# Router logits from the raw residual with scaled weights, routing by pairwise comparison, three token tiles routed inside the last projection tile, and h2 made by GpSimd

## The reference

```python
x = x + gate1 * mixed                      # mixed = (merged branches) @ w_o
h2 = rms_norm(x, norm2_g) * (1 + scale2) + shift2
x = x + gate2 * hier_moe(h2, p)
# hier_moe(h):
gl = x @ w_rg + b_rg                       # 4 groups, top 1
el = x @ w_re + b_re                       # 16 experts, 4 in a group, top 2 of the chosen group
topv = topv / sum(topv); weights = gp_sel * topv
g = einsum('nd,edf->nef', x, w_e_gate); u = einsum('nd,edf->nef', x, w_e_up)
act = silu(g) * u * combine[:, :, None]
out = einsum('nef,efd->nd', act, w_e_down)
```

## Time and profile before

| | us |
|---|---|
| three runs | 738.91, 739.37, 739.41 (median 739.37) |
| profiled execution, first to last instruction (span) | 737.5 |
| last projection group ends, the add of its tile starts | 505.6 |
| `slot_i` written | 531.3 |
| first gathered tile transposed | 537.7 |
| high matmuls of slot 0, of slot 1 start | 540.8, 548.7 |

### The profile page before, as it was taken

The page is one execution under the profiler, slowest core; times in us unless marked ns, Lnnn a source line. Parts: engine busy times, 40 slices in busy tenths (PEclk is TensorE's granted clock), DMA queues, the critical chain, the costliest instruction groups (busy, mean ns, idle before and its releaser), DMA issues.

```text
span 737.5 us, 11172 instructions
## 1 busy us (share of the span) xinstructions
PE 703.8 (95%) x4440; PEld 611.4 (83%) x4440; DVE 544.1 (74%) x785; ACT 344.3 (47%) x454; POOL 201.3 (27%) x84
## 2 busy tenths in 40 slices
PE   5899999999999999999999999998989999999985
PEld 2499999999998899999999998886368888877752
DVE  3547999999768765955556563555799999888877
ACT  4552223433333444446365121134387888777622
POOL 4004321322200000000000000000239999797560
PEclk9999999999999999999999999999599999999998
DMA  9954145445625345512325326266958999999783
GB/s 321 377 169 141 59 172 172 172 172 173 218 83 114 31 120 123 116 61 61 111 64 166 114 71 217 80 245 218 412 195 335 394 406 404 393 357 361 262 283 144
DMA packets 75607, 149.10 MB, mean 202 GB/s; under 512 B 11302, under 2 KB 54626, under 8 KB 68836
## 3 DMA queue, kind: packets, MB, share of 16 engines
q1 hardware_dynamic: 61572, 125.28, 49.4%
q10 hardware_dynamic: 10096, 12.63, 4.8%
q0 software_dynamic: 3888, 10.49, 4.2%
HBM read 138.29 MB, written 20.05 MB: 215 GB/s over the span
## 4 chain that ended last, share of the span: by engine, by line
PE 76%; DMA 9%; DVE 4%; issue 3%; ACT 3%; POOL 2%; SPq 2%; POOLq 0%; DVEq 0%; ACTq 0%
PE psum L990 36%; PE psum L1241 8%; PE psum L1283 7%; PE psum L505 3%; PE psum L925 3%; PE psum L506 3%; PE psum L511 3%; DMA down_raw<-in_w_e_down 2%; DMA w_more<-in_w_ada 2%; PE psum L1188 2%; DMA xg<-h_d,slot_b 1%; PE psum L1432 1%; SPq L791 1%; PE psum L1118 1%; PE psum L1009 1%
## 5 line engine op out<-in xcount | busy, mean ns | idle before, releaser
L990 PE MATMUL psum<-hh,w_h 128*128 128x320 f32 x608 | 144.4, 319 | 0.2 <-issue 0.2
L990 PE MATMUL psum<-hh,w_l 128*128 128x320 f32 x608 | 138.5, 309 | 0.0
L990 PE MATMUL psum<-hl,w_h 128*128 128x320 f32 x608 | 138.4, 309 | 0.0
L2014 DVE SCALAR_TENSOR_TENSOR psum<-conv,taps,psum 128x760 f32<-128x760 f32 x103 | 104.5, 1015 | 3.5
L990 PEld LDWEIGHTS psum<-hh,w_h 128*128 128x128 f32 x608 | 99.8, 188 | 5.4 <-issue 3.1
L990 PEld LDWEIGHTS psum<-hl,w_h 128*128 128x128 f32 x608 | 101.6, 188 | 0.0
L990 PEld LDWEIGHTS psum<-hh,w_l 128*128 128x128 f32 x608 | 101.5, 188 | 0.0
L717 POOL TENSOR_TENSOR down_l<-down_raw,down_h 128x2048 fp32r<-128x2048 f32 x16 | 87.8, 5486 | 20.8 <-ACT down_h L1787 20.3
L683 POOL TENSOR_TENSOR ob<-obh,toff 128x260 bf16<-128x260 f32 x1 | 2.0, 1995 | 332.1 <-DVE obh L591 332.1
L2300 DVE TENSOR_TENSOR w_l<-w_raw,w_h 128x2048 fp32r<-128x2048 f32 x26 | 77.0, 2966 | 11.7 <-ACT w_h L1793 11.7
L917 POOL TENSOR_TENSOR w_l<-w_raw,w_h 128x2048 fp32r<-128x2048 f32 x9 | 41.8, 4640 | 144.1 <-ACT w_h L1468 144.1
(11 more groups left out here) (384 smaller groups left out, 1403.4 us busy)
## 6 DMA issues: line engine op xcount, KB each, us to landing
w_raw<-in_w_in SPq DMA_DIRECT2D x20, 1024.0 KB, 6.7
down_raw<-in_w_e_down SPq DMA_DIRECT2D x17, 1024.0 KB, 12.3
w_raw<-in_w_ada SPq DMA_DIRECT2D x16, 1024.0 KB, 9.2
w_raw<-in_w_e_gate SPq DMA_DIRECT2D x13, 1024.0 KB, 7.8
w_raw<-in_w_e_up SPq DMA_DIRECT2D x13, 1024.0 KB, 11.3
w_more<-in_w_ada SPq DMA_DIRECT2D x8, 1024.0 KB, 10.5
y_d<-yy ACTq DMA_DIRECT2D x15, 512.0 KB, 8.2
y_d<-in_x_sample SPq DMA_DIRECT2D x12, 512.0 KB, 8.1
```

Of the source, the lines that this page charges most:

```text
L990: mm = pe.matmul(psum[:, p + q, 0:HALF], w, r[:, k, q * HALF:(q + 1) * HALF], start=(k == 0 and x == 0), stop=(k == KT - 1 and x == 2))
L2014: ins = dve.scalar_tensor_tensor(out=after, in0=src, scalar=w, in1=before, op0=MUL, op1=ADD)
```

## The change

- Router logits come from the transposes of x2 itself. `wrs` is `wr` times the scale row (now loaded as a column for each partition), the shift row's share is worked out once for both token kinds (`shift_terms`, `shift_rows`, `lgc`), and rstd multiplies the finished logits (`scaled_logits`).
- h2 is made by POOL (times scale row, then plus shift row, 1024 columns each) with a pass of ACT between (times rstd, `h2_scale`). POOL stores the last of the five tiles itself, on its own queue, and both the first gather and SP's load of down weights 2 wait for that store.
- Ranks come from pairwise comparisons with a tie term (`choose`). Tiles 0 to 2 are routed during the last projection group, tiles 3 and 4 after it.
- The slot list is one matmul per pick with the token's number as value (`oav`, float32 words), no longer two columns.
- SP loads the down weights of slot 0 when all logits are done, those of slot 2 when the last h2 tile is stored, and those of slot 1 when the slots' row weights are done.
- POOL waits for gather 0 to land before it issues gather 1. PE transposes gather 1 between the high and the low matmuls of slot 0, no longer ahead of them, and the second half of gate2's spreading stands behind the transposes of gather 0.
- 11 `keep_clock` matmuls ahead of the logits are gone, and 2 are left of the 3 ahead of slot 0. The load of `norm_final_g` moves into slot 2.

```diff
+    def x2_out(act, t, q):
         if t >= 2:
             act.wait_ge(lgt_pe, t - 1)
+        act.wait_ge(h2_pe, 2 * t + q + 1)
+        act.activation(h2t[:, t % 2, 4 * q:4 * q + 4, :],
+                       psum[:, 5 + q, :].rearrange("p (k n) -> p k n", k=4), ACT.Copy).then_inc(h2_ev, 1)
...
+    def choose(dve, then, t0, t1):
+
+        n = t1 - t0
+        sets = lg[:, t0:t1, :].rearrange("p t (s e) -> p (t s) e", e=GE)
+        ahead = lead[:, 0:5 * n, :, :]
+        wide = [P, 5 * n, GE, GE]
+        then(dve.tensor_tensor(ahead, sets.unsqueeze(2).to_broadcast(wide), sets.unsqueeze(3).to_broadcast(wide), SUB))
+        flat_sets = lead[:, 0:5 * n, :, :].rearrange("p a i j -> p a (i j)")
+        then(dve.tensor_tensor(flat_sets, flat_sets,
+                               tau[:, :, :].rearrange("p i j -> p (i j)").unsqueeze(1).to_broadcast([P, 5 * n, GE * GE]),
+                               ALU.is_gt))
+        then(dve.tensor_reduce(rank[:, 0:n, :, :].rearrange("p t s e -> p (t s) e"), ahead, AX, ADD))
+        then(dve.tensor_scalar(ghot[:, 0:n, :], rank[:, 0:n, 0, :], 0.0, None, ALU.is_equal))
...
@@ POOL, experts_pool @@
+        pool.wait_ge(mod_in, 16 * 6)
+        for t in range(NT):
+            v = min(t, 1)
+            left = 0
+            if t == NT - 1:
+                left = 512
+                pool.wait_ge(x2_left, X2_LEFT + NT)
+                pool.tensor_tensor(h2[:, t, 0:left], x2[:, t, 0:left], bsc[:, v, 0:left], MUL)
+            pool.wait_ge(x2_done, t + 1)
+            pool.tensor_tensor(h2[:, t, left:D], x2[:, t, left:D], bsc[:, v, left:D], MUL).then_inc(h2_half, 1)
+            pool.wait_ge(h2_scaled, H2_SCALED + t + 1)
+            pool.tensor_tensor(h2[:, t, :], h2[:, t, :], bsh[:, v, :], ADD).then_inc(h2_dve, 1)
+        pool.wait_ge(h2_dve, NT)
+        pool.dma_start(h2_d[(NT - 1) * P:NT * P, :], h2[:, NT - 1, :]).then_inc(h2_last_st, 16)
+        pool.wait_ge(h2_last_st, 16)
+        pool.wait_ge(h2_st, 16 * NT)
         pool.wait_ge(slots, 1)
...
-        for b in range(3):
+        known_gather(0)
+        pool.wait_ge(xg_in[0], 16)
+        for b in range(1, 3):
             known_gather(b)
...
@@ SP @@
+        h2_store(3)
         gate_up(1, 1, own(1))
-        for t in range(3, NT):
-            h2_store(t)
+        sp.wait_ge(lg_done, 2)
+        down_weights(0, 0, own(0))
         gate_up(2, 0, own(2))
-        sp.wait_ge(x2_done, NT)
+        sp.wait_ge(h2_st, 16 * NT)
+        sp.wait_ge(h2_last_st, 16)
+        down_weights(2, 0, own(2))
+        sp.wait_ge(rt_pe, 4)
         down_weights(1, 1, own(1))
-        sp.wait_ge(lg_done, 1)
-        down_weights(0, 0, own(0))
-        sp.wait_ge(h2_st, 16 * (NT + 1))
-        down_weights(2, 0, own(2))
...
@@ PE, the projection's loop @@
+                    if half and t == NT - 1 and k == 1:
+                        pe.wait_ge(lgc_done, LGC_DONE)
+                        for early in range(3):
+                            last = token_logits(early)
+                        last.then_inc(lg_done, 1)
+                    if half and t and k == 3:
+                        turn_x2(t - 1, 0)
+                        turn_x2(t - 1, 1)
+                    if half and t == NT - 1 and k == 5:
+                        turn_x2(t, 0)
+                        early_counts()
                 mm.then_inc(wo_done, 1)
-                if half and t >= 2:
-                    turn_h2(t - 2)
-                if half and t >= 3:
-                    logits(t - 3)
-        keep_clock(7, 8)
...
@@ PE, slot 0
+            if first:
+                pe.wait_ge(e_hi, 2)
+                for k in range(KT):
+                    if k % 4 == 0:
+                        pe.wait_ge(x_lo, k // 4 + 1)
+                    for x in (xh, xl):
+                        pe.matmul(psum[:, s, :], x[:, s, k, :], both(wh, k), start=(k == 0 and x is xh), stop=False)
+                row_weights()
+                turn_x(1 - s, u + s, b + 1)
```

506 lines of the change are left out of this document (331 added, 175 removed).

## The result

The change made the kernel slower: 749.03 us median of four runs (747.24 to 749.78) against 739.14 for the kernel before in runs beside them, a ratio of 1.0128 with a 95% interval of 1.0098 to 1.0158. The forecast was 742.8 with a range of 737.6 to 746.5. The direction was right; 9.9 us were lost where 3.4 were forecast, and the time lies above the range.

The account below looks back on a forecast made before the run. PE is busy from slot 1's start on, so that start, set by gather 0's landing and the way from there, bounds the end. Span 737.5 + 2.9 + 0.5 = 740.9, plus 1.9 for runs: 742.8 us, range 737.6 to 746.5.

Parts of the forecast that it names:

- S: Start of slot 1's high matmuls on PE; forecast at 551.6 instead of 548.73, 2.9 us later.
- G: Landing of gather 0; forecast at 536.8, 0.7 us earlier than before, range 532.4 to 539.5.
- The projection's end and the slot list: Last projection group ends at about 511.2 instead of 505.6; `slot_i` stands at 526.7 against 531.33, gaining 4.6 us.
- The store: POOL's store of the last h2 tile: issued at 521.6, takes 9 us (4 to 12), lands at 530.7.
- 5.8 MB at 0.41 MB per us: Traffic SP has issued since 515.5, claimed to keep the queues deep until 532 while the last h2 tile is stored.
- Gather 0: Goes out after the last h2 tile's store lands, with 1 MB of down weights beside it; taken as 6 us.
- The quick rival: Queues share evenly at 521.6 to 532: store lands at 526.5, gather 0 at 532.3; 737.6 us, chance 0.17.
- G to S: From gather 0's landing to slot 1's high matmuls: 14.8 us instead of 11.2, `sil` after 12.7; a loss of 3.6.
- a rival of its own: Clock still at 1.2 GHz when gather 0 lands, so transposes, spreading and high matmuls take 3.3 us more; 746 us, chance 0.23.
- T: Start of gather 0's transposes on PE, a point used in reading the traces.
- What else was removed: Other removals were covered; `norm_final_g`'s 512 KB costs 0.5 us (at most 1.3), extra small SP transfers at worst 1 us.
- what the experts absorb (nothing): From slot 1 on PE is busy 10.00 of 10 us, so the end moves with slot 1's start.

Follow-up runs that it names:

- e2_pool_off: Changed kernel with GpSimd's h2 passes cut to one column, scale and shift rows left out of the experts' input; 747.59 us, ratio 1.0107 to before.
- f3_all_off: Changed kernel with one-column GpSimd passes (scale, shift left out), slot 0's old order, SP's slot 2 weights held for gather 0, six clock matmuls; 740.0 us, ratio 1.0007.
- h2_v4: Changed kernel: VectorE makes h2 except tile 3, slot 0's old order, SP's weights held, no clock matmuls before gather 0's transposes, second low part earlier; 740.0 us, ratio 1.0018.
- e3_split: Changed kernel with each GpSimd h2 pass cut into instructions of 128 columns; 752.64 us, ratio 1.0169 to before.
- f1_before_slot0: Kernel before, with only the change's slot 0 order: gather 1 issued after gather 0 lands, row weights and its transposes behind the high matmuls; 744.98 us, ratio 1.0101.

## Why the prediction was wrong

S came 6.8 us later than forecast. By the trace 3.1 of it came with the landing of the store, 0.9 with the issue of gather 0, 1.2 with its landing, and 1.6 between G and S.

*The projection's end and the slot list: the step that failed.* The working has POOL's passes only as time on POOL (2.3 us each) and VectorE's steps as if it ran alone. It put what a running pass does to VectorE at nothing, without a reason. Measured, the projection ended 2.6 us and slot_i 6.9 us later than forecast; with the passes off both came within 0.8 us of the forecast. The counting of matmuls and steps was right, the contention was missing. Taking it away alone did not bring the time back (`e2_pool_off`), as gather 0 then took 2.5 us longer; only with order and hold put right as well did the loss go (`f3_all_off`, `h2_v4`). It could have been read in the trace before, where GpSimd's passes meet VectorE's in the experts (VectorE, then GpSimd):

```profile
547.44 2.28 DVE L2300 TENSOR_TENSOR third_l<-third_raw,w_h 128x2048 fp32r<-128x2048 f32 x1
...
551.90 4.49 DVE L2300 TENSOR_TENSOR w_l<-w_raw,w_h 128x2048 fp32r<-128x2048 f32 x1 [0.65 <-ACT w_h L1793]
```

```profile
548.89 5.33 POOL L717 TENSOR_TENSOR down_l<-down_raw,down_h 128x2048 fp32r<-128x2048 f32 x1 [6.06 <-ACT down_h L1787]
```

The same instruction takes 2.28 us alone and 4.49 here: GpSimd's pass ends at 554.22, and 554.22 + 2.28 is 556.5; it ends at 556.39. The Trainium skill, page "SBUF — State Buffer", section "SBUF: two separate sides", says the same: VectorE and GpSimd share a pair of ports as an exclusive lock, for the whole instruction, which touches VectorE where it has two scratchpad inputs (against a GpSimd instruction that reads the scratchpad) or runs in a two-port mode. The rows here agree: the copy from PSUM at 518.69 took 0.41 inside a pass, `lead` waited; in which mode the one-hot matrices run, no row says. And the hold goes both ways: the pass at 548.89 starts inside VectorE's of 547.44 and takes 5.33 us, where one alone takes 4.64.

*The store.* Its landing, the unknown, was well taken: 8.6 against 9, with a part of luck, as it was allowed 4 to 12, and that weights queued on SP stretch it is seen in one run only. The working's 5.8 MB at 0.41 MB per us would last until 529.6, not 532; only the depth of the queues was taken from it. The store went out 3.6 us late, because the wait of VectorE's `lead` ran through PE's counts and ScalarE's scale of tile 3 back to POOL. It landed at 58.0, together with slot_i (57.8), so both chains now end at G.

*Gather 0.* Two small terms were wrong: the 0.9 us from the store's landing to the issue was left out, and the landing took 7.2, not 6. With 3.1 from the store this is the 5.2 us by which G was late. The quick rival (fair shares between queues) did not come: the store took 6.8 to 9.5 us in all fifteen runs that have it. Gather 0 took 5.1 to 5.8 in the runs with SP held where its landing was read, and 5.6 in `e3_split`, where it was issued late. That it is stretched by SP's weights, as the prediction had it, is shown (7.2 against 5.5 by the hold alone).

*G to S.* The chain over ScalarE was right to 0.1 us (`sil` at G + 12.7). From there it took 3.8 us and not 2.1: 0.9 of the difference because `act` waited for the low parts that stand behind the late tables, 0.7 because slot 1's first transposes ran at the clock of 0.50. The prediction gave the low clock a rival of its own, 0.23, at G. It came at G, where it cost 0.6 us (transposes 1.72 instead of 1.13), and at S, where the prediction did not look for it. From T the runs take the way apart in steps, each by one trace: order back 2.6 us, VectorE's pass back 2.0, and then 11.8 is left against 11.1. The right 12.7 is luck in part: in `f1_before_slot0` the same order, without the spreading behind the transposes, has `sil` 15.2 us behind T, 13.9 without its table load.

*What else was removed.* The 0.5 us for `norm_final_g` can't be told: S to the end is 0.9 us longer in the trace after, and 187.9 to 191.4 us in the variants that leave the tables in place. The step on what the experts absorb (nothing) was right: 9.6 us at S are 10.6 at the end.

What stays open: why executions of one kernel differ by 2.5 to 8.5 us, since each trace shows only one, and what sets the 8.3 to 9.5 us of the store.

## What to carry to other kernels

Before work is moved to GpSimd, list what VectorE does meanwhile: each of its instructions with two scratchpad inputs, and its one-hot passes, costs its own time plus the rest of the running pass, however small it is. A 16-column instruction can cost as much as the longest pass (4.61 us here). An engine's idle time ahead of a wait is a resource: a 2.3 us pass that stood behind the wait cost 2.0 us, and ahead of it nothing that the trace shows. Where two engines' work is reordered, follow the whole cycle (gather, copies, weight parts, activations) and not just the wait that is removed, and read a run's gain at the end, since S early and the end late was seen twice.
